# Third attention: query tiles three to eight among its units, a step of them between scores and transposes

## What is computed

```python
def swa_sink_mixer(h, w_in, b_in, sinks, w_out, b_out):
    proj = h @ w_in + b_in
    q, k, v = jnp.split(proj, [16 * 64, (16 + 2) * 64], axis=-1)
    ...                                   # k, v: own block of 128 tokens and the one before
    s = jnp.einsum('bnqkgd,bnskd->bnkgqs', q, kb) * 64 ** -0.5
    s = jnp.where(valid, s, -jnp.inf)     # band of 128, causal
    mx = jnp.maximum(jnp.max(s, axis=-1, keepdims=True), sink)
    e = jnp.exp(s - mx)
    p = e / (jnp.sum(e, axis=-1, keepdims=True) + jnp.exp(sink - mx))
    o = jnp.einsum('bnkgqs,bnskd->bnqkgd', p, vb)
    return o.reshape(B, T, 16 * 64) @ w_out + b_out
```

## Time and profile before

| | us |
|---|---|
| median of 3 runs | 2469.01 (2467.21 to 2470.68) |
| span of the profiled execution | 2468.0 |
| PE busy in it | 2423.7 (98%) |
| ACT, POOL, DVE busy | 1079.6, 972.3, 936.0 |
| first query product `sq1` starts | 1941.1 |
| the attention's first scores | 1979.25 |
| its last output tile written | 2039.2 |

### The profile page before, as it was taken

One profiled execution on the slowest core, in us unless ns is written; L12 is line 12 of the kernel. 1 busy time (PEld: TensorE's weight loads), 2 busy tenths in 40 slices (PEclk: granted clock), 3 DMA queues, 4 the chain that ended last, 5 costly groups with the idle time before them and its releaser, 6 DMA issues.

```text
span 2468.0 us, 36248 instructions
## 1 busy us (share of the span) xinstructions
PE 2423.7 (98%) x11990; PEld 2004.0 (81%) x11990; DVE 936.0 (38%) x2051; ACT 1079.6 (44%) x1917; POOL 972.3 (39%) x484
## 2 busy tenths in 40 slices
PE   8999999999999999999999999999999999999998
PEld 6888888888778978888887978788888797788886
DVE  7976322211477753222214243321211773311212
ACT  7565443432347754444335534432332583432321
POOL 4821444444331124444443413444443423444441
PEclk9999999999999999999999999999999999999999
DMA  4300333333420013233332312233333202233331
GB/s 154 116 30 18 90 97 101 94 102 105 128 69 10 1 35 94 93 102 93 103 102 79 103 39 81 77 95 95 100 94 94 69 18 69 86 101 95 94 94 68
DMA packets 57866, 202.75 MB, mean 82 GB/s; under 512 B 7072, under 2 KB 7968, under 8 KB 57392
## 3 DMA queue, kind: packets, MB, share of 16 engines
q1 hardware_dynamic: 54864, 196.02, 26.2%
q10 hardware_dynamic: 2912, 5.55, 0.6%
HBM read 199.44 MB, written 2.10 MB: 82 GB/s over the span
## 4 chain that ended last, share of the span: by engine, by line
PE 41%; issue 14%; POOL 7%; ACT 1%; DVE 1%; POOLq 0%; DVEq 0%; ACTq 0%
PE bank L764 36%; POOL w_lo L618 7%; PE bank L1008 1%; PE bank L967 1%; PE bank L979 1%; ACT h_hi L1492 1%; PE bank L1372 0%; PE bank L1353 0%; ACT gained L1495 0%; PE bank L1367 0%; PE bank L793 0%; PE bank L1055 0%; PE bank L881 0%; PE bank L770 0%; PE bank L786 0%
## 5 line engine op out<-in xcount | busy, mean ns | idle before, releaser
L618 POOL TENSOR_TENSOR w_lo<-w_raw,w_hi 128x1024 fp32r<-128x1024 f32 x368 | 883.3, 2401 | 1197.7 <-ACT w_hi L1449 1188.1
L764 PE MATMUL bank<-h_hi,w_hi 128*128 128x512 f32 x1648 | 650.5, 395 | 7.2 <-DVE tmp L2476 2.1
L764 PE MATMUL bank<-h_lo,w_hi 128*128 128x512 f32 x1648 | 642.2, 390 | 0.0
L764 PE MATMUL bank<-h_hi,w_lo 128*128 128x512 f32 x1648 | 642.2, 390 | 0.0
L1449 ACT ACTIVATE w_hi<-w_raw 128x1024 fp32r<-128x1024 f32 x368 | 386.8, 1051 | 242.7 <-PE bank L764 214.0
L764 PEld LDWEIGHTS bank<-h_hi,w_hi 128*128 128x128 f32 x1648 | 309.8, 188 | 82.3 <-issue 5.9
L764 PEld LDWEIGHTS bank<-h_hi,w_lo 128*128 128x128 f32 x1648 | 309.7, 188 | 65.2
L764 PEld LDWEIGHTS bank<-h_lo,w_hi 128*128 128x128 f32 x1648 | 309.9, 188 | 65.0 <-issue 2.2
L764 PE MATMUL bank<-mact_hi,w_hi 128*128 128x512 f32 x512 | 199.3, 389 | 1.7 <-DVEq L2342 1.7
L764 PE MATMUL bank<-mact_hi,w_lo 128*128 128x512 f32 x512 | 199.2, 389 | 0.0
L764 PE MATMUL bank<-mact_lo,w_hi 128*128 128x512 f32 x512 | 199.2, 389 | 0.0
(11 more groups left out here) (403 smaller groups left out, 3489.3 us busy)
## 6 DMA issues: line engine op xcount, KB each, us to landing
w_raw<-in_weights SPq DMA_DIRECT2D x368, 512.0 KB, 3.6
out<-x ACTq DMA_DIRECT2D x8, 256.0 KB, 2.1
x<-in_xT SPq DMA_DIRECT2D x4, 256.0 KB, 6.8
x<-in_xT ACTq DMA_DIRECT2D x4, 256.0 KB, 7.4
memx<-in_memT SPq DMA_DIRECT2D x1, 1024.0 KB, 9.8
cmp_w1k<-in_cmp_w ACTq DMA_DIRECT2D x1, 1024.0 KB, 5.6
cmp_w1v<-in_cmp_w ACTq DMA_DIRECT2D x1, 1024.0 KB, 7.5
rope_c<-in_rope_c SPq DMA_DIRECT2D x1, 256.0 KB, 8.4
```

The source lines that it names most:

```text
L618: nc.gpsimd.tensor_tensor(w_lo[:, t % RING, :], w_raw[:, t % RAW, :], w_hi[:, t % RING, :].bitcast(F32), ALU.subtract).then_inc(lo_ready, 1)
L764: r = nc.tensor.matmul(out, a, b, start=first and n == 0, stop=last and n == 2)
```

## The change

Query tiles `sq2` to `sq7` are no longer computed ahead of the attention. Their 48 steps (six tiles by eight k, three matmuls each) stand among its units: four steps ahead of the first scores, one behind each of the first four units' scores, and one in each of the steps 0 to 39, behind the scores and ahead of the transposes. All six tiles use bank 1 alone (`sq1` bank 3, `sq0` bank 2), so the scores are left with three banks and a look-ahead of four units instead of five. PE may begin a tile only when DVE has moved the one before out of bank 1 (`query_moved`). The copies to `q_stage2` go, and PE reads `q_swa`. The scale goes to the keys; the bias is added in the rounding (ACT) and in the rest (DVE), and DVE's operation for bias and scale of the queries is gone. ACT's rounding of weight chunks and POOL's rests for them, six of the latter in quarters of 256 columns, are also placed among the units. The attention's loops are written out.

```diff
-OWN["sq0"] = 2
+OWN.update({"sq0": 2, "sq1": 3}, **{f"sq{j}": 1 for j in range(2, KT)})
...
-def look_ahead(kind):
-    return 5 if kind.startswith("swa") else 4
+LOOK_AHEAD = 4
+def swa_unit(n):
+    return (f"swa{n // 32}", 0, n % 8, n % 32 // 8) if n < 64 else None
+def query_step(s):
+    return f"sq{2 + s // KT}", s % KT
+QUERY_STEPS = (KT - 2) * KT
+EARLY_STEPS = 8
... POOL
+            end = CHUNK["sq1"] + AHEAD + 1
+            rests(start, end)
+            for head in range(2 * SWA_PAIRS):
+                add_sink(*swa_unit(TT * head))
+                if head in (0, 2, 4, 6, 8, 10):
+                    rest_in_quarters(end)
+                    end += 1
... PE
+                    def query_products(s):
+                        name, k = query_step(s)
+                        if k == 0:
+                            chunk_ready(CHUNK[name])
+                            pe.wait_ge(query_moved, int(name[2]) if s else 1)
+                        r = three(of(name)[:, :], slot(CHUNK[name], k), (h_hi[:, k, :], h_lo[:, k, :]), k == 0, k == KT - 1)
...
+                    for s in range(4):
+                        query_products(s)
                     pe.wait_ge(k_split, 13)
+                    for n in range(4):
+                        if n < 2:
+                            pe.wait_ge(query_moved, n + 1)
+                        scores(*swa_unit(n))
+                        query_products(4 + n)
+                    for n in range(2):
+                        transposes(*swa_unit(n))
+                    for n in range(2 * 4 * SWA_PAIRS):
+                        if swa_unit(n + LOOK_AHEAD):
+                            scores(*swa_unit(n + LOOK_AHEAD))
+                        if EARLY_STEPS + n < QUERY_STEPS:
+                            query_products(EARLY_STEPS + n)
+                        if swa_unit(n + 2):
+                            transposes(*swa_unit(n + 2))
+                        values(*swa_unit(n))
... ACT
+                    for n in range(2 * 4 * SWA_PAIRS):
+                        if swa_unit(n + LOOK_AHEAD - 1):
+                            exponentials(*swa_unit(n + LOOK_AHEAD - 1))
+                        if swa_unit(n + 2):
+                            move_transposed(*swa_unit(n + 2))
+                        done = 2 + n // 8
+                        if n % 8 in (1, 2) and done < KT:
+                            round_query(done, [n % 8 - 1])
+                        if n % 8 == 4 and done < KT:
+                            split_ahead(CHUNK[f"sq{done}"])
... DVE
+                    for n in range(2 * 4 * SWA_PAIRS):
+                        if swa_unit(n + LOOK_AHEAD):
+                            maximum(*swa_unit(n + LOOK_AHEAD))
+                        output(*swa_unit(n))
+                        done = 2 + n // 8
+                        if n % 8 == 0 and done < KT:
+                            move_query(done)
+                        if n % 8 in (2, 3) and done < KT:
+                            rest_of_query(done, [n % 8 - 2])
```

More of the change, by code:

```diff
@@ L209, in attention_stream @@
             begin(lambda u: (kind, pair, u, 0))
-        unrolled = int(n == 0 and first is not None)
-        if unrolled:
-            first(per, lambda u: (kind, pair, u, 0) if u < per else (kind, pair, u - per, 1))
         if pairs > 1:
-            with eng.Fori(unrolled, pairs - 1) as i:
+            with eng.Fori(0, pairs - 1) as i:
                 pair_of_heads(per, lambda u: (kind, pair, u, i) if u < per else (kind, pair, u - per, i + 1))
@@ L619, in rest, with rest_in_quarters @@
                                         w_hi[:, t % RING, :].bitcast(F32), ALU.subtract).then_inc(lo_ready, 1)
+            def rest_in_quarters(t):
+                pool.wait_ge(hi_ready, t + 1)
+                for n in range(0, KT * P, 2 * P):
+                    part = slice(n, n + 2 * P)
+                    r = nc.gpsimd.tensor_tensor(w_lo[:, t % RING, part], w_raw[:, t % RAW, part], w_hi[:, t % RING, part].bitcast(F32), ALU.subtract)
+                r.then_inc(lo_ready, 1)
             def rests(t, end):
@@ L744, in _ @@
                 start = norms(start, names)
+            end = CHUNK["sq1"] + AHEAD + 1
[5 more added lines that the diff above has]
+                    end += 1
+            start = norms(end, ["mlppre1"])
             rests(start, N_CHUNKS)
@@ L1600, in attention_begin @@
             def attention_begin(at):
-                for u in range(look_ahead(at(0)[0]) - 1):
+                for u in range(LOOK_AHEAD - 1):
                     exponentials(*at(u))
@@ L2271, in attention_begin @@
             def attention_begin(at):
-                if at(0)[0] == "swa0":
-                    hold_sink(0, 0)
-                for u in range(look_ahead(at(0)[0])):
+                for u in range(LOOK_AHEAD):
                     maximum(*at(u))
@@ L2279, in unit_of_pair @@
             def unit_of_pair(u, at):
-                later = u + look_ahead(at(u)[0])
+                later = u + LOOK_AHEAD
                 if at(later):
@@ new lines, in rest_of_query @@
+                    def rest_of_query(j, heads=(0, 1)):
+                        dve.wait_ge(query_moved, j + 1)
+                        for hh, (part, hi, lo) in enumerate(both_heads("swa0", j, sq_q[:, j, :])):
+                            if hh in heads:
+                                dve.wait_ge(q_rounded, 24 + 2 * j + hh + 1)
+                                bias = col("swa_b_q", j)[HD * hh:HD * hh + HD, :]
+                                nc.vector.scalar_tensor_tensor(lo, part, bias, hi.bitcast(F32), ALU.add, ALU.subtract).then_inc(q_split, 1)
@@ new lines, in _ @@
+                    scaled_by_root("sk", sk[:, :])
+                    biased(0, sk[:, :], col("swa_bk"), SCALE)
+                    scaled_by_root("sv", diag[:, :])
+                    biased(1, diag[:, :], col("swa_bv"))
+                    move_query(0)
+                    rest_of_both(9, sk[:, :], *k_swa)
+                    rest_of_query(0)
+                    move_query(1)
+                    hold_sink(0, 0)
+                    for n in range(LOOK_AHEAD):
+                        maximum(*swa_unit(n))
```

126 lines of the change are left out of this document (52 added, 74 removed).

## The result

| | before | after |
|---|---|---|
| median | 2467.21 us (2464.96 to 2470.68, 5 runs) | 2484.15 us (2483.65 to 2486.51, 5 runs) |
| span of the profiled execution | 2468.0 | 2481.9 |
| ratio of the times, 95% interval | | 1.0069, 1.0057 to 1.0082 |

The change makes the kernel slower by 0.69%, 16.9 us. I had forecast slower by 0.28%, 7.0 us, with a range that ended at 2481.5. The direction was right; the forecast size is less than half of the measured one. The profiled spans are only 13.9 us apart, since the profiled execution of the kernel before had a lower mean granted clock (0.996) than its executions of median length: at 0.998 its spans are 2464.2 to 2465.5 us (measured beside e7), and the changed kernel's 2482.0 and 2482.4. What follows takes the profiles apart, so it accounts for 13.9 us.

A forecast was written before the change was run, and what follows sets the result against it. PE bounds the kernel, without holes in the even part. Span 2468.0 - 6.6 (old start, waits) + 3.0 (new start) + 6.6 (holds) + 4.0 (last 24 steps) = 2475.0 us; median 1.0 above, 2476.0, range 2470.5 to 2481.5.

The forecast's parts named there:

- scores 3 and the last step of `sq2` by 1953.4: New start of the third attention: PE was to have issued both by 1953.4 us, ahead of unit 1's transposes at 1954.6.
- 3.0 us of idle time: New start, 1949.3 to 1956.4 us: PE has 4.1 us of work, so 3.0 us idle (2 to 4).
- it has caught up before a unit misses it: Chunks in steps 4, 12, 20, 28 and 36 delay DVE, but with 1.50 us steps this costs nothing.
- What bounds it: Even part of the third attention: PE has no holes that products could fill; a step has about 0.02 us of waits.
- "faster" rival: Product matmuls hide weight loads: one more a step saves 4.4 us, three save 13.2; chance 0.06.
- well below 1.45: Sign for hidden loads: scores in steps 13 to 37 well under 1.45 us apart, instead of about 1.50.
- The step with a product: Product step 0.68 us, whole step 1.50; the 0.02 us waits in 40 steps go, 0.7 us saved.
- The start: Start of the third attention: the old loss of 5.9 us goes, 3.0 us of new PE idle time comes.
- The holds: Steps 8, 16, 24 and 32: PE waits 1.65 us each until DVE empties bank 1, 6.6 us in all.
- From unit 44 to the end: Last 24 steps, without products: look-ahead 0.8 us, `sq7` on ACT 1.2, chunk `mix1.2` 2.0; sum 4.0 (2 to 6).
- at several places: Clock rival: PE's clock falls in or behind several holds, half clock over 3.4 us costing 1.7 us each; chance 0.05.
- at all five places: Clock rival in full: falls at the start and all four holds cost 8.5 us, giving 2484.5 us.

The follow-up runs named there:

- e7: e2 and e3 combined, plus a fourth score bank from unit 40 and twelve product steps ahead of the loop instead of eight: ratio 0.9990, 2464.71 us.
- s1: Changed kernel with `sq2`'s move ahead of the second query's rests on DVE: first step of `sq3` 2.0 us sooner; one profile.
- e2: Changed kernel with query tiles alternating between two product banks, 1 and 7: ratio to the kernel before 1.0020, span 2469.5 us.
- e3: Changed kernel with POOL's rest of a weight chunk behind the second of two heads' sums instead of the first: ratio to the kernel before 1.0036.
- s2: Changed kernel with POOL's second rest of the start made in four quarters: first step of `sq3` 0.9 us sooner; one profile.
- e1: Changed kernel with DVE's move of a query tile ahead of the last output: ratio to the kernel before 1.0052, span 2477.6 us.
- e4: Changed kernel with the edits of e1 and e3 together: ratio to the kernel before 1.0035, span 2470.0 us.

## Why the prediction was wrong in size

Between the transposes of `sv` and of the outputs the forecast had 7.0 us of loss, measured were 15.0. The step that failed most is the start, "scores 3 and the last step of `sq2` by 1953.4" and with it the 3.0 us of idle time; in the holds it is "it has caught up before a unit misses it". By the forecast's own steps:

- **What bounds it: right.** PE had no holes, and moving products gave nothing. The "faster" rival fell: a step was 1.51 us, not "well below 1.45".
- **The step with a product: 1.2 us too low.** A product step took 0.70 us among the units, not 0.68 (1967.90 to 1968.60; or four steps in 6.05 us, less 0.817 each). The rest of the step stayed at 0.81 us, so the 0.02 us a step that I took for waits of the old even part did not go, and the 0.7 us credited for them did not come.
- **The start: 2.4 us too low.** Forecast 15.7 us from `sv`'s transposes to the first step of `sq3`, measured 18.1. The half clock at 1941 has no part in it: unit 5's scores came 19.2 us behind those transposes with it, and in after's second profile without it. Four things were missed: scores 3 need unit 0's bank and thus the first exponential (1954.61, not by 1953.4); the maximum of unit 3 stands ahead of the second query's rests; two rests with a bias are 1.53 us, two such roundings 1.47, not 1.4 and 1.29; and the fourth key rest ended at 1949.0, not with POOL's instruction at 1948.4. s1 (2.0 us less) and e2 (unit 5's scores at 16.6 instead of 19.2 us) show from two sides that the move's place on DVE and the one bank set it.
- **The holds: 1.8 us too low.** The chain of 1.65 was nearly right (e3: 1.54). The step that failed is "with a step of 1.50 us it has caught up before a unit misses it": DVE does not catch up, for the late inversion stands directly ahead of the hold, and POOL's order, put at nothing here, cost 0.56 us in each (e3).
- **From unit 44 to the end: 4.6 against 4.0, but by other shares** (25.30 us against 20.73). Look-ahead 0.09 us a step at the end of after (0.91 against 0.817), 1.8 in 19 steps where I had 0.8; POOL 1.5 (e3) where I had 2.0; the rest, about 1.3, is left for ACT's rounding and split, for which I had 1.2 (the rounding alone). No run priced it by itself.
- **The clock: 1.6 us.** A fall behind holds was in my range once; I had put "at several places" at 0.05. In five profiles of kernels whose four holds are 2.1 us (after three times, s1, s2) each had one or two falls behind one of them, six in twenty holds. In e1, e3 and e4 none of twelve shorter holds had one behind it (two had one behind the start's 2.5 us), and in the five profiles with two banks there is no fall in the attention. Six of twenty against none of twelve is suggestive and no more: chance alone gives such a split about one time in twenty. The time of 2484.15 us beside the rival "at all five places", 2484.5, is coincidence, since the profile has one such fall.

2.4 + 1.8 + 1.6 + 1.2 + 0.6 is 7.6 of the 8.0 us missing; 0.4 stay unassigned. Behind it, 1.2 us went with the fall at the attention's end, which I had assumed to stay. The last 3.0 us between the forecast's and the measured difference of the medians are the slow execution that I started from: I put the median 1.0 us above the profiled span, while the five runs' median is 0.8 below it, so by the granted clocks above I had counted half clocks of that one execution as the kernel's normal time.

The Trainium skill, SBUF — State Buffer, section on the two separate sides, says that GpSimd's operations and DVE's with two SBUF inputs hold a shared port pair for a whole instruction. The trace of after agrees: three key rests of 0.69 us alone took 6.30 beside POOL's two. A move, which reads one of its two inputs from PSUM, is not held: in the kernel before the one at 1979.44 us lay wholly inside a rest of POOL (1978.71 to 1981.09) and kept its 0.69.

```profile
1942.70 6.30 DVE L2192 TENSOR_TENSOR k_swa_lo<-sk,k_swa_hi 64x512 fp32r<-64x512 f32 x3
...
1943.11 2.53 POOL L627 TENSOR_TENSOR w_lo<-w_raw,w_hi 128x1024 fp32r<-128x1024 f32 x1 [5.15 <-ACT w_hi L1496]
...
1946.04 2.41 POOL L627 TENSOR_TENSOR w_lo<-w_raw,w_hi 128x1024 fp32r<-128x1024 f32 x1 [0.40 <-ACT w_hi L1496]
```

The Trainium skill, TensorE: Matmul & The Clock Gate, section on psum-queue depth-cycling, tells of a clock that falls again and again by short idle times between groups of matmuls. The falls behind holds, at a granted clock of 0.50 to 0.52, look like that; which hold they hit, these runs don't show.

## What to carry to other kernels

Filling one engine with work from elsewhere gives nothing where it has no holes, and each buffer taken for it must be priced by the wait that the buffer had hidden: here one product bank cost 8.4 us in four holds (2.2 of them by POOL's order) and 2.7 at the start (2.0 of them also by DVE's order, s1), one score bank 0.09 to 0.12 us a unit. With all of these waits taken out the new order was level with the old one, not faster. Follow a wait upstream through every in-order queue: the hold was shortened by 0.6 us by either of two edits and by 1.7 by both. Take a second profile before crediting half a clock to a cause, and compare the profiled execution's granted clock with that of the median run before forecasting from it.

## What the runs showed of the hardware

- Half clock for 3.4 us behind a hold of 2.1 us came in six of twenty cases, at other holds in other executions of the same kernel, and cost 1.6 us (2.81 and 1.84 us for two steps instead of 1.49 and 1.60).
- A fall can be free: the one at 1940.7 made the products ahead of the first scores slower, but what came behind them was set by DVE and not later for it.
- Quarters instead of one long POOL instruction let DVE's rests in between: a rest started 1.6 us sooner, and both then took longer (four quarters 4.19 us instead of the 2.81 of those at 1967.69 in after, two rests 2.26 instead of 1.53).
